# Attention scores of both key-value heads issued alternately on their own 64 rows, the bias table added by products with the identity, transposed probabilities in two buffers

## The reference, cut to what matters

```
kb, vb = band(k), band(v)                      # block n and the block before it
scores = einsum('bnqhgd,bnkhd->bhgnqk', qb, kb) * (ATTN_HEAD_DIM ** -0.5)
dist = WINDOW + qi - ki
scores = scores - slopes * dist                # ALiBi
scores = where(valid, scores, -inf)
m = maximum(scores.max(axis=-1), sink)
p = exp(scores - m)
probs = p / (p.sum(axis=-1) + exp(sink - m))
out = einsum('bhgnqk,bnkhd->bnqhgd', probs, vb)
```

## Time and profile before

| | us |
|---|---|
| median of 3 runs | 2129.72 (2129.05 to 2130.49) |
| the profiled execution's own time | 2124.94 |
| its span in the trace | 2123.2 |
| PE busy in the span | 1980.7 (93%) |
| DVE busy | 1638.5 (77%) |
| ACT busy | 1314.7 (62%) |
| first exponential of attention to last head in `mix` | 282.20 to 373.22 |

### The profile page before, as it was taken

One profiled execution on the slowest core, in us unless ns is written; L12 is line 12 of the kernel. 1 busy time (PEld: TensorE's weight loads), 2 busy tenths in 40 slices (PEclk: granted clock), 3 DMA queues, 4 the chain that ended last, 5 costly groups with the idle time before them and its releaser, 6 DMA issues. The chain is left out here.

```text
span 2123.2 us, 39981 instructions
## 1 busy us (share of the span) xinstructions
PE 1980.7 (93%) x11114; PEld 1695.3 (80%) x11115; DVE 1638.5 (77%) x2237; ACT 1314.7 (62%) x1912; POOL 653.4 (31%) x781
## 2 busy tenths in 40 slices
PE   7999978788985899999999999999999999999993
PEld 6887867776874789788897888978897888978882
DVE  5333176895666789889898898989898898988985
ACT  5221244663433667767677676778677676776775
POOL 3100000320225233425333253345334253342621
PEclk9999989999995999999999999999999999999997
DMA  5222120003236989989898998989898998989988
GB/s 189 66 80 70 40 100 1 11 21 122 74 96 205 365 249 356 295 301 338 271 360 288 305 336 272 360 289 371 281 363 286 308 332 272 359 290 309 333 272 304
DMA packets 265229, 506.50 MB, mean 239 GB/s; under 512 B 38550, under 2 KB 39574, under 8 KB 264916
## 3 DMA queue, kind: packets, MB, share of 16 engines
q1 hardware_dynamic: 243000, 457.91, 62.3%
q0 software_dynamic: 22176, 47.90, 8.8%
HBM read 466.50 MB, written 39.22 MB: 238 GB/s over the span
## 5 line engine op out<-in xcount | busy, mean ns | idle before, releaser
L1925 DVE TENSOR_TENSOR wlo<-raw,whi 128x1024 fp32r<-128x1024 f32 x774 | 956.1, 1259 | 64.8 <-ACT whi L1372 59.4
L1372 ACT ACTIVATE whi<-raw 128x1024 fp32r<-128x1024 f32 x775 | 844.3, 1116 | 141.8 <-PE ps L1057 102.4
L1055 PE MATMUL ps<-xT,whi 128*128 128x320 f32 x1920 | 503.9, 349 | 6.3 <-DVE wlo L1925 5.8
L1057 PE MATMUL ps<-xT,wlo 128*128 128x160 f32 x1920 | 455.7, 237 | 0.0
L1055 PEld LDWEIGHTS ps<-xT,whi 128*128 128x128 f32 x1920 | 362.7, 189 | 10.0 <-DVE wlo L1925 6.2
L1057 PEld LDWEIGHTS ps<-xT,wlo 128*128 128x128 f32 x1920 | 368.7, 192 | 0.5
L651 PE MATMUL ps<-whi,xT 128*128 128x512 f32 x544 | 218.2, 401 | 1.2 <-DVE xT L1948 1.2
L653 PE MATMUL ps<-whi,xT 128*128 128x512 f32 x544 | 213.2, 392 | 0.0
L651 PE MATMUL ps<-whi,aT 128*128 128x512 f32 x512 | 212.8, 416 | 0.3 <-DVE aTl L1986 0.3
L652 PE MATMUL ps<-wlo,xT 128*128 128x512 f32 x544 | 212.6, 391 | 0.0
L653 PE MATMUL ps<-whi,aTl 128*128 128x512 f32 x512 | 201.0, 393 | 0.0
(11 more groups left out here) (321 smaller groups left out, 3544.6 us busy)
## 6 DMA issues: line engine op xcount, KB each, us to landing
raw<-in_w SPq DMA_DIRECT2D x780, 512.0 KB
raw<-in_w_in SPq DMA_DIRECT2D x16, 512.0 KB
xs<-in_x SPq DMA_DIRECT2D x8, 512.0 KB, 10.3
raw<-in_w_out SPq DMA_DIRECT2D x8, 512.0 KB
mix<-in_x SPq DMA_DIRECT2D x8, 512.0 KB, 3.7
h_d<-h SPq DMA_DIRECT2D x8, 512.0 KB
acc_d<-mix SPq DMA_DIRECT2D x8, 512.0 KB
mix<-acc_d SPq DMA_DIRECT2D x8, 512.0 KB, 6.6
```

The costliest lines, as they stand in the source:

```text
L1055: pe.matmul(o2, wh[:, a, cols], xT2[:, :, k, 0:JOB_T], start=q == 0 and a == 0, stop=False, skip_group_check=True)
L1057: m = pe.matmul(o, wl[:, a, cols], xT2[:, 0, k, 0:JOB_T], start=False, stop=q == QUARTERS - 1 and a == 1, skip_group_check=True)
L1372: act.activation(parted(slot(whis, s)), paired(raw_slot(s), s), ACT.Copy).then_inc(split_hi, 1)
L1925: dve.tensor_tensor(parted(slot(wlos, s)), paired(raw_slot(s), s), parted(slot(whis, s).bitcast(F32)), ALU.subtract).then_inc(split_lo, 1)
```

## The change

Scores. `scores(n)` now holds both heads: for each query head i the product of kv 0 (rows 0 to 63, banks 0 and 1) and that of kv 1 (rows 64 to 127, banks 2 and 3) are issued one after the other, so neighbouring products lie on different rows and in different banks.

Table. Nothing is added on DVE any more. Ahead of the scores PE writes the table itself into the four banks: `table(n, kv)` is two products of an identity (`identr`, fp32r) with 512 columns of `alibi` (now fp32r too), and the scores accumulate on it (`start=False`). DVE's `find_max(b)` takes the maximum from PSUM, negated, joins it with the negated sink in one small operation and releases ACT; the sink's argument follows with a semaphore of its own. ACT's exponentials read PSUM and write `score`.

Buffers. `probT` has one half for each kv, so values(b) has only to be done before copy(b+2). PE's list for a block n is now: turn(2n), table(n+1, 0), table(n+1, 1), scores(n+1), turn(2n+1), values(2n), values(2n+1).

Start. `alibi_set(1)` stands behind chain 4 of unit 5, the two first `find_max` behind chains 6 and 7, the scores of block 0 wait for chain 3 and the tables, and `split(6, 3)` moves behind the first two `exps` on ACT and ahead of the first copy on DVE.

```diff
-            def scores(b):
-                n, kv = divmod(b, 2)
-                if b >= 2:
-                    pe.wait_ge(score_added, b - 1)
+            def table(n, kv):
+                b = 2 * n + kv
+                if n == 0:
+                    pe.wait_ge(tables_set, kv + 2)
+                else:
+                    pe.wait_ge(exped, b - 1)
+                lo = P if n == 0 else 0
+                for two in range(2):
+                    h = GROUP * kv + 2 * two
+                    pe.matmul(ps[:, 2 * kv + two, :].rearrange("p (i k) -> p i k", i=2)[:, :, lo:], identr[:, :],
+                              alibi[:, h:h + 2, lo:], start=True, stop=False, skip_group_check=True)
+
+            def scores(n):
                 lo = P if n == 0 else 0
                 for i in range(GROUP):
-                    m = pe.matmul(ps[:, 2 * kv + i // 2, (i % 2) * 256 + lo:(i % 2) * 256 + 256],
-                                  aq[64 * kv:64 * kv + 64, i, n * P:(n + 1) * P],
-                                  ak[64 * kv:64 * kv + 64, n * P + lo:n * P + 256],
-                                  start=True, stop=True)
-                m.then_inc(scored, 1)
+                    for kv in range(NKV):
+                        rows = slice(64 * kv, 64 * kv + 64)
+                        m = pe.matmul(ps[:, 2 * kv + i // 2, (i % 2) * 256 + lo:(i % 2) * 256 + 256],
+                                      aq[rows, i, n * P:(n + 1) * P], ak[rows, n * P + lo:n * P + 256],
+                                      start=False, stop=i % 2 == 1, skip_group_check=True)
+                        if i == GROUP - 1:
+                            m.then_inc(scored, 1)
...
+            for n in range(NT):
+                probs_turn(2 * n)
+                if n + 1 < NT:
+                    for kv in range(NKV):
+                        table(n + 1, kv)
+                    scores(n + 1)
+                probs_turn(2 * n + 1)
+                for kv in range(NKV):
+                    values(2 * n + kv)
...
             def exps(b):
                 kv = b % 2
                 act.wait_ge(maxed, b + 1)
+                if b >= 2:
+                    act.wait_ge(probs_turned, 2 * b - 2)
                 lo = P if b < 2 else 0
                 for i in range(GROUP):
-                    m = act.activation(score[:, kv, i, lo:], score[:, kv, i, lo:], ACT.Exp,
+                    m = act.activation(score[:, kv, i, lo:],
+                                       ps[:, 2 * kv + i // 2, (i % 2) * 256 + lo:(i % 2) * 256 + 256], ACT.Exp,
                                        bias=stat[:, 1, b, i:i + 1], accum_out=stat[:, 3, b, i:i + 1])
                 m.then_inc(exped, 1)
+                act.wait_ge(sink_arg, b + 1)
                 act.activation(stat[:, 4, b, :], stat[:, 2, b, :], ACT.Exp).then_inc(sinked, 1)
...
+            for n in range(NT):
+                for kv in range(NKV):
+                    probs_copied(2 * n + kv)
+                if n + 1 < NT:
+                    for kv in range(NKV):
+                        exps(2 * n + 2 + kv)
...
+            def find_max(b):
                 n, kv = divmod(b, 2)
                 dve.wait_ge(scored, b + 1)
-                if b >= 2:
-
-                    dve.wait_ge(probs_turned, 2 * b - 2)
                 lo = P if n == 0 else 0
-                s = score[:, kv, :, lo:]
-                link(dve.tensor_tensor(s, ps[:, 2 * kv:2 * kv + 2, :].rearrange("p a (i k) -> p (a i) k", i=2)[:, :, lo:],
-                                       alibi[:, GROUP * kv:GROUP * kv + GROUP, lo:], ALU.add))
...
+                s = ps[:, 2 * kv:2 * kv + 2, :].rearrange("p a (i k) -> p (a i) k", i=2)[:, :, lo:]
+                link(dve.tensor_reduce(stat[:, 0, b, :], s, AX, ALU.max, negate=True))
+                dve.tensor_tensor(stat[:, 1, b, :], stat[:, 0, b, :], nsinks[:, GROUP * kv:GROUP * kv + GROUP],
+                                  ALU.min).then_inc(maxed, 1)
+                dve.wait_ge(maxed, b + 1)
+                dve.tensor_tensor(stat[:, 2, b, :], sinks[:, GROUP * kv:GROUP * kv + GROUP], stat[:, 1, b, :],
+                                  ALU.add).then_inc(sink_arg, 1)
...
+            split(6, 3)
+            for n in range(NT):
+                probs_copied(2 * n)
+                if n > 0:
+                    heads_scaled(2 * n - 1)
+                for kv in range(NKV):
+                    denominator(2 * n + kv)
+                if n + 1 < NT:
+                    find_max(2 * n + 2)
+                probs_copied(2 * n + 1)
+                if n + 1 < NT:
+                    find_max(2 * n + 3)
+                heads_scaled(2 * n)
             heads_scaled(2 * NT - 1)
```

More of the change, by code:

```diff
@@ L126, in build @@
     mix = at("mix", A, [P, NT, D])
-    alibi = at("alibi", A + 32 * KB, [P, NQ, 2 * P])
+    alibi = at("alibi", A + 32 * KB, [P, NQ, 2 * P], F32R)
+    identr = at("identr", A + 58 * KB, [P, P], F32R)
     score = at("score", A + 40 * KB, [P, 2, GROUP, 2 * P])
-    probT = at("probT", A + 48 * KB, [P, 2, GROUP, P])
+    probT = at("probT", A + 48 * KB, [P, NKV, 2, GROUP, P])
     hpx = at("hpx", A + 52 * KB, [P, T])
@@ L223, in build @@
     sinks = rest("sinks", [P, NQ])
+    nsinks = rest("nsinks", [P, NQ])
     lbl = rest("lbl", [P, 2, HH])
@@ L772, in _, with values @@
                     m.then_inc(probs_turned, 1)
-                if b + 2 < 2 * NT:
-                    scores(b + 2)
+            def values(b):
+                n, kv = divmod(b, 2)
                 pe.wait_ge(pT_act, b + 1)
@@ L781, in _ @@
                     if n > 0:
-                        pe.matmul(o, probT[:, 0, i, :], av[:, n - 1, :], start=True, stop=False)
-                    m = pe.matmul(o, probT[:, 1, i, :], av[:, n, :], start=n == 0, stop=True)
+                        pe.matmul(o, probT[:, kv, 0, i, :], av[:, n - 1, :], start=True, stop=False)
+                    m = pe.matmul(o, probT[:, kv, 1, i, :], av[:, n, :], start=n == 0, stop=True)
                 m.then_inc(heads_done, 1)
+            pe.wait_ge(*taken(5, 3))
+            for kv in range(NKV):
+                table(0, kv)
+            scores(0)
+            pe.wait_ge(*taken(5, 7))
+            for n in range(NT):
[7 more added lines that the diff above has]
+                    values(2 * n + kv)
             pe.wait_ge(heads_out, 2 * NT)
@@ L1192, in _ @@
                         act.activation(hgs[:, c % 2, :], ps[:, c, :], ACT.Sigmoid).then_inc(taken_act, 1)
-                split(n + 1, 3)
+                if n < 5:
+                    split(n + 1, 3)
                 if n == 3:
@@ L1218, in _, with probs_copied @@
             exps(1)
-            for b in range(2 * NT):
+            split(6, 3)
+            def probs_copied(b):
                 if b < 2:
                     act.sem_inc(pT_act, 1)
[L1222 to L1228, removed]
+                    return
+                act.wait_ge(probs_turned, 2 * b + 1)
+                act.wait_ge(heads_done, b - 1)
+                act.activation(probT[:, b % 2, 0, :, :], ps[:, 4, :].rearrange("p (i n) -> p i n", i=GROUP),
+                               ACT.Copy).then_inc(pT_act, 1)
+            for n in range(NT):
[4 more added lines that the diff above has]
+                        exps(2 * n + 2 + kv)
             squares = [0]
@@ L1588, in _ @@
                             dve.wait_ge(const_set, 2)
+                            dve.tensor_copy(identr[:, :], ident[:, :])
                             alibi_set(0)
-                        elif c == 5:
-                            add_bias(0)
-                split(n + 1, 3)
+                        elif c == 4:
+                            alibi_set(1)
+                        elif c == 6:
+                            find_max(0)
+                        elif c == 7:
+                            find_max(1)
+                if n < 5:
+                    split(n + 1, 3)
                 if n == 1:
@@ L1621, in heads_scaled, with probs_copied @@
                                   ALU.mult).then_inc(heads_out, 1)
-            alibi_set(1)
-            add_bias(1)
-            for b in range(2 * NT):
+            def probs_copied(b):
                 dve.wait_ge(probs_turned, 2 * b + 2)
-                if b >= 1:
-                    dve.wait_ge(heads_done, b)
-                dve.tensor_copy(probT[:, 1, :, :], ps[:, 5, :].rearrange("p (i n) -> p i n", i=GROUP)).then_inc(pT_dve, 1)
-                denominator(b)
-                if b >= 1:
-                    heads_scaled(b - 1)
-                if b + 2 < 2 * NT:
-                    add_bias(b + 2)
+                if b >= 2:
+                    dve.wait_ge(heads_done, b - 1)
+                dve.tensor_copy(probT[:, b % 2, 1, :, :],
+                                ps[:, 5, :].rearrange("p (i n) -> p i n", i=GROUP)).then_inc(pT_dve, 1)
+            split(6, 3)
+            for n in range(NT):
+                probs_copied(2 * n)
+                if n > 0:
```

(4 more changed lines are left out.)

30 lines of the change are left out of this document (10 added, 20 removed).

## The result

| | us |
|---|---|
| median after, 4 runs | 2101.68 (2100.28 to 2103.50) |
| median before, 4 runs on the same chip | 2129.39 (2128.54 to 2130.49) |
| ratio | 0.9873, interval 0.9861 to 0.9885 |
| span of the profiled execution after (before) | 2101.9 (2123.2) |

The kernel became 27.7 us faster.

What follows compares the result with a forecast made beforehand. Attention was taken to be bound by a loop through several engines, its period falling from 10.74 to 8.8 us. Attention ending 18.2 us sooner, taken from 2129.7 (4.8 above the profiled execution), gave 2111.7, range 2108 to 2121.

Steps and rivals of the forecast that it cites:

- What bounds: Attention: no engine is full, a loop through several sets the 10.74 us period; a handoff shift reaches the end one to one.
- Alternated scores: Scores of a block: products on different rows run side by side, 1.84 us (lower end) against 3.68 if alternation gives nothing.
- the slot of 0.23: Scores: 0.23 us added to PE's sum for the lone first instruction, which has no other head's instruction to run beside.
- Rivals 1 and 3: Scores: 1, alternation brings nothing, 2123.6, chance 0.12; 3, each change of rows makes PE stand, 2132.3, chance 0.04.
- Mode change: Ahead of the scores: PE stands 0.17 us, now once a block instead of twice.
- Table: Table products on PE: 512 columns each, starting every 0.23 us, so 0.46 us a head and 0.92 a block.
- The period: Two steps of attention: 8.82 us along PE, 8.83 along the data, taken as 8.8 instead of 10.74.
- The start: Start of attention: exps(3) end at 296.7 instead of 298.6, gain 2.0 us, 1 us of it uncertain.
- The end: End of attention: exps(15) end at 349.5, squares at 357.8 against 376.04, 18.2 us less.
- The sum: Whole kernel: 2124.94 less 18.2 is 2106.7; the median's 4.8 above the profiled execution carried over gives 2111.7.
- Bounds: Whole kernel: range 2108 to 2121; the forecast's own range, 2109 to 2116.7, took a period of 8.5 to 9.2.

Runs made afterwards that it cites:

- second trace: The kernel before, run and traced again with no edit: median 2128.53 us, ratio 0.9998; the traced execution took 2130.29 us.
- filled kernel: The kernel before with four thrown-away products of 512 columns on PE in the wait of each even step: 2123.65 us, ratio 0.9981.

## Why the prediction fell short, step by step

**What bounds.** Right in the main: attention was a loop through several engines. That a shift of the handoff goes through to the end one to one held for the first pair of traces (21.8 and 21.3), but not in general: from the handoff to the first expert job the traces of these kernels show between 305.7 and 311.4 us.

**Alternated scores.** Right, at the lower end: sixteen instructions in 2.00 us, and 1.93 until the next turn starts. By the pairs of starts both instructions of a product ran beside the other head's, so there is no lone first one and the slot of 0.23 was not needed. Rivals 1 and 3 fell with it: 2.96 us even without alternation, and no stand at a change of rows. The Trainium skill, TensorEngine Tiling (Array Packing), section Tiling Modes, says that a change of the tile inside a mode needs no drain; the starts 6 ns apart agree.

**Mode change.** Half seen. The prediction took 0.17 once a block from the earlier trace rows; PE stands 0.36 on the way in and 0.33 on the way out.

**Table.** 0.46 a head was nearly right: the four products and the mode change reach from 320.64 to 321.75, 1.11 us against 0.92 and 0.17, with a short wait for the exponentials inside.

**The period.** Forecast 8.8, measured 8.33. Along the data: from the end of exps(2n+1) to the scores 0.83 (forecast 0.67), until DVE starts 2.10 (2.26), until exps(2n+3) start 3.59 (3.9), until they end 1.81 (2.0, of which the PSUM source is 0.1). Along PE: turns 1.72 (1.92), table with its mode change 1.11 (1.09), scores 1.93 (2.07), values 3.57 (3.74). The structure was right, and most terms were 0.1 to 0.3 too large. A likely reason, not tested by itself, is that they were read as end-to-start distances in a kernel where the engines stood before each group. Six periods give 2.8 us.

**The start.** The copy behind exps(3) starts at 296.01, and unit 4 had begun 1.1 us later than in the trace before (182.7 against 181.6): 3.8 us gained, from unit 4 on, where 2.0 were forecast. 1.1 of the difference is that later unit 4, the rest are smaller terms: the second half of the table took 1.42 us, not 1.80, and the scores of block 1 with their tables 5.2 us in all.

**The end.** Right: from the end of exps(15) to the handoff 8.2 us, forecast 8.3.

**The sum.** This is the step that failed: "The median lies 4.8 above the profiled execution, so I forecast 2129.7 - 18.2". It took the 4.8 for something that the change would leave alone. Without it the forecast would have been 2106.7, already below the range. (2129.7 - 18.2 is also 2111.5, not 2111.7.) With the terms above right (2.8 and 1.8 more, 1.1 less for the later unit 4) the forecast of 18.2 would have been near the 21.8 of the first two traces; the other 6 us of the 27.7 lie in this step.

What the runs showed in its place: an ordinary execution of the kernel before loses more time, and a good part of it in what the change removes. The second trace is 5.4 us longer: 2.3 in attention (one more period at the lower clock 1.4, the start 0.6, the last step 0.3), 1.6 ahead of unit 4 and 1.5 behind the handoff. In all, the clock takes 4.4 us of attention (filled kernel against the second trace; 5.1 by the medians), of which the prediction counted 1.6: it read one fall in its trace, while the last step there took 4.51 us from copy to copy where the filled kernel takes 3.15. Against this ordinary execution attention ends 25.65 us sooner: start 4.9 with what lay ahead of it, six periods 17.4 (67.42 to 50.01), tail 3.4. Another 2.1 us lie between the handoff and the first expert job (308.2 to 306.1); to what they belong isn't shown. That the clock falls in the gaps is shown by filling them; what exactly it reacts to is not.

**Bounds.** The range reached 3.7 us below the forecast. It held a period of 8.5 at least, and nothing for a carried difference of 4.8 that might go away.

## What to carry to other kernels

Ahead of a sum against a profile, look where the profiled execution lies among the timed ones; if it is the fastest, trace another, ask what the others lose and whether the change removes just that, instead of carrying the difference over. When two variants are compared by their times alone, look also at a time from the start of the stage to its end: here 4.4 us of the difference between two traces lay in stages that neither edit touches. Two groups of fp32 products that use half of the rows each are worth issuing product by product in turn, on their own rows and banks: they ran fully side by side. Don't add up parts that were taken back one at a time: alternation, second buffer and table cost 8.9, 13.8 and 10.8 us here, 33.5 together, more than the whole 27.7, since each of the loops through a stage must be short for the period to be short.

## What the runs showed of the hardware

PE started a product out of the order of the program when it lay on other rows: at 326.626 us, ahead of three instructions that stand before it (the profile models the ends of products, so only starts are used). The Trainium skill, TensorE: Matmul & The Clock Gate, Part 3: Packing small matmuls — row/col tiling, describes products as starting and ending in program order; the trace of the scores one head after the other does not agree, and decides here.

Two fp32 products over 256 columns on rows 0 to 63 and 64 to 127 started 6 ns apart, a further pair each 216 ns, so that sixteen instructions took 2.00 us where eight took 1.99.

PE's granted clock fell in a stage where PE was busy 9.6 of 10.7 us, and in the trace with the rest filled by products whose result nobody reads it did not: 5.1 us of the whole by the medians, 4.4 in attention by the traces. A filling of 3.6 us at the start, behind which PE stood 1.7 us, did not hold it.
